# An encoder layer on one core: the first phase in six pieces instead of five, half of the turned input copied by ScalarE, late constants sent for after the first weights

## The reference

```python
cond = jax.nn.silu(c)
mod = cond @ w_ada[l] + b_ada[l]
sh1, sc1, gt1, sh2, sc2, gt2 = jnp.split(mod, N_MOD, axis=-1)
hn = modulated_rms_norm(h, sh1, sc1)     # rms_norm(x) * (1 + sc1) + sh1
proj = hn @ w_in[l]
```

## Time and profile before

| | us |
|---|---|
| median of 3 runs | 2613.78 |
| lowest, highest | 2613.31, 2613.84 |
| profiled execution | 2611.63 |
| its span | 2610.0 |
| PE busy in the span | 2517.7 (96%) |
| DVE busy | 1477.6 (57%) |
| ACT busy | 903.4 (35%) |

### The profile page before, as it was taken

One profiled execution on the slowest core, in us unless ns is written; L12 is line 12 of the kernel. 1 busy time (PEld: TensorE's weight loads), 2 busy tenths in 40 slices (PEclk: granted clock), 3 DMA queues, 4 the chain that ended last, 5 costly groups with the idle time before them and its releaser, 6 DMA issues.

```text
span 2610.0 us, 34653 instructions
## 1 busy us (share of the span) xinstructions
PE 2517.7 (96%) x11920; PEld 2060.3 (79%) x11920; DVE 1477.6 (57%) x1917; ACT 903.4 (35%) x1274; POOL 201.7 (8%) x278
## 2 busy tenths in 40 slices
PE   4999999999999899989999999999999999999997
PEld 4777787787787678868888888888888888888786
DVE  6837678678678584474444444444444444444454
ACT  4334424424424334342222222222222222222344
POOL 3401121111121021000000000000000000000000
PEclk7999999999999899999999999999999999999998
DMA  9933454454454355323333333323333333333233
GB/s 353 324 109 113 131 161 128 133 158 130 135 157 129 109 145 153 97 73 98 96 96 88 104 97 96 96 88 98 104 96 97 96 89 96 100 96 96 87 95 130
DMA packets 431728, 318.20 MB, mean 122 GB/s; under 512 B 12950, under 2 KB 403905, under 8 KB 431169
## 3 DMA queue, kind: packets, MB, share of 16 engines
q1 hardware_dynamic: 401712, 212.19, 28.2%
q0 software_dynamic: 29184, 104.87, 12.4%
q10 hardware_dynamic: 785, 0.51, 0.1%
HBM read 313.33 MB, written 4.19 MB: 122 GB/s over the span
## 4 chain that ended last, share of the span: by engine, by line
PE 89%; DVE 6%; issue 2%; ACT 1%; DMA 1%; POOL 0%; DVEq 0%; ACTq 0%; POOLq 0%
PE pw L1474 23%; PE pw L1476 22%; PE pw L1475 22%; PE pw L1458 2%; PE pw L1460 2%; PE pw L1459 2%; PE pd L1791 2%; PE pd L1768 1%; PE pd L1783 1%; DMA ka<-in_w_ada_dram 1%; DVE w_lo L969 1%; PE pd L1731 1%; PE pd L1808 1%; PE pd L1803 1%; DVE ada_acc L985 1%
## 5 line engine op out<-in xcount | busy, mean ns | idle before, releaser
L1474 PE MATMUL pw<-act_hi,w_hi 128*128 128x512 f32 x1984 | 793.8, 400 | 3.8 <-DVE w_lo L969 3.0
L969 DVE TENSOR_TENSOR w_lo<-raw,w_hi 128x1024 fp32r<-128x1024 f32 x426 | 524.0, 1230 | 481.4 <-ACT w_hi L573 475.0
L1476 PE MATMUL pw<-act_hi,w_lo 128*128 128x512 f32 x1984 | 774.3, 390 | 0.0
L1475 PE MATMUL pw<-act_lo,w_hi 128*128 128x512 f32 x1984 | 773.1, 390 | 0.0
L573 ACT ACTIVATE w_hi<-raw 128x1024 fp32r<-128x1024 f32 x426 | 450.2, 1057 | 542.9 <-PE pw L1476 444.6
L1474 PEld LDWEIGHTS pw<-act_hi,w_hi 128*128 128x128 f32 x1984 | 373.2, 188 | 90.2 <-issue 16.4
L1475 PEld LDWEIGHTS pw<-act_lo,w_hi 128*128 128x128 f32 x1984 | 373.2, 188 | 81.4 <-issue 6.9
L1476 PEld LDWEIGHTS pw<-act_hi,w_lo 128*128 128x128 f32 x1984 | 372.8, 188 | 78.8
L1474 PE MATMUL pw<-mh_hi,w_hi 128*128 128x512 f32 x704 | 276.1, 392 | 3.0 <-DVE w_lo L969 3.0
L1476 PE MATMUL pw<-mh_hi,w_lo 128*128 128x512 f32 x704 | 274.2, 389 | 0.0
L1475 PE MATMUL pw<-mh_lo,w_hi 128*128 128x512 f32 x704 | 274.0, 389 | 0.0
(11 more groups left out here) (291 smaller groups left out, 2469.8 us busy)
## 6 DMA issues: line engine op xcount, KB each, us to landing
raw<-in_w_up_dram SPq DMA_DIRECT2D x172, 512.0 KB, 4.0
ada_w<-in_w_ada_dram POOLq DMA_DIRECT2D x128, 512.0 KB, 4.6
raw<-in_w_in_dram SPq DMA_DIRECT2D x84, 512.0 KB, 3.9
raw<-in_w_down_dram SPq DMA_DIRECT2D x64, 384.0 KB, 3.4
raw<-in_w_down_dram SPq DMA_DIRECT2D x64, 320.0 KB, 3.2
raw<-in_w_out_dram SPq DMA_DIRECT2D x32, 512.0 KB, 4.6
DD<-in_w_ada_dram POOLq DMA_DIRECT2D x9, 512.0 KB, 8.0
EG<-in_w_ada_dram POOLq DMA_DIRECT2D x9, 512.0 KB, 6.7
```

The source lines that it names most:

```text
L969: V.tensor_tensor(w_lo[slot][:], raw[slot][:], w_hi[slot][:].bitcast(F32), ALU.subtract).then_inc(lo_made.sem, 1)
L1474: M(bank, w_hi[slot][:, k, :], hi[:, k0 + k, :], start=first, stop=False)
L1475: M(bank, w_hi[slot][:, k, :], lo[:, k0 + k, :], start=False, stop=False)
L1476: ins = M(bank, w_lo[slot][:, k, :], hi[:, k0 + k, :], start=False, stop=last)
```

## The change

The first piece of four feature tiles becomes two pieces of two, so there are six. The copies of x blocks 2 and 3 move from VectorE to ScalarE, with signals of their own. The late constants are issued after the gate weights. `normed` for tiles 0 and 1 stands behind step i = 10 of the second piece, the low halves of the first two weight units behind its steps 8 and 9. The products on tiles 0 and 1 are made for units 0 and 1 only, the rest of these units when tiles 2 and 3 are there; unit 2 takes all four tiles at once. Four signals of x become one that counts steps.

```diff
-PIECES = ((0, 4), (4, 8), (8, 12), (12, 14), (14, 16))
+PIECES = ((0, 2), (2, 4), (4, 8), (8, 12), (12, 14), (14, 16))
...
-            sp.dma_start(cst[:, C_FIRST:C_N], A["shape_constants"][:, C_FIRST:C_N]).then_inc(more_in, 16)
...
             sp.dma_start(wba, w_in[:, COL_BA:COL_BA + 32].rearrange("(k p) n -> p k n", p=P)).then_inc(ba_in, 16)
+            sp.dma_start(cst[:, C_FIRST:C_N], A["shape_constants"][:, C_FIRST:C_N]).then_inc(more_in, 16)
...
+            def x_block(b):
+
+                for q in range(4):
+                    act.wait_ge(*xt_sum.after(0, 4 * b + q + 1))
+                    nc.scalar.activation(x_feat[:, 4 * q:4 * q + 4, b * P:(b + 1) * P], blocks(pd[q]), ACT.Copy).then_inc(x_copied.sem, 1)
+
+            x_block(2)
             split(0, 0, ahead=False)
+            x_block(3)
             split(0, 1, ahead=False)
...
-            act.wait_ge(ba_in, 16)
-            nc.scalar.activation(wba_hi[:], wba, ACT.Copy).then_inc(ba_split.sem, 1)
             act.wait_ge(*x_turned.after(0))
+            act.wait_ge(*x_copied.after(0))
...
             first_halves(0)
+            act.wait_ge(ba_in, 16)
+            nc.scalar.activation(wba_hi[:], wba, ACT.Copy).then_inc(ba_split.sem, 1)
+            first_halves(1)
             first_split(2)
             first_split(3)
-            first_halves(1)
+            first_halves(2)
...
-                if i in (2, 4, 6, 8):
-                    x_block((2, 4, 6, 8).index(i))
-                if i in (10, 11):
-                    low(0, i - 10)
-
-            def ahead(j, lows):
+                if i in (5, 8):
+                    x_block((5, 8).index(i))
+
+            def ahead(j, lows, at_row=2):
...
-                    if 2 <= i < 2 + len(tiles):
-                        normed(tiles[i - 2])
-                    if i == 6 and j == 1:
+                    if at_row <= i < at_row + len(tiles):
+                        normed(tiles[i - at_row])
+                    if i == 13 and j == 1:
...
-            ahead(1, {7: 2, 11: 3})
-            ahead(2, {5: 4, 8: 5, 12: 6})
-            ahead(3, {5: 7, 9: 8, 13: 9})
-            ahead(4, {5: 10})
+            ahead(1, {8: 0, 9: 1}, at_row=10)
+            ahead(2, {7: 2, 11: 3})
+            ahead(3, {5: 4, 8: 5, 12: 6})
+            ahead(4, {5: 7, 9: 8, 13: 9})
+            ahead(5, {5: 10})
...
                 for q in range(4):
-                    if b:
+                    if b == NB - 1:
+                        pe.wait_ge(*x_copied.after(0, q + 1))
+                    elif b:
                         pe.wait_ge(*x_turned.after(0, 4 * (b - 1) + q + 1))
...
-            for j in range(3):
+            first_unit(0, 0, 2, end=False)
+            first_turned(1, TURNED_ROWS[0])
+            first_unit(1, 0, 2, end=False)
+            first_turned(1, TURNED_ROWS[1])
+            first_sums(1)
+            first_unit(0, 2, 4)
+            first_turned(2, TURNED_ROWS[0])
+            first_unit(1, 2, 4)
+            first_turned(2, TURNED_ROWS[1])
+            ba_part(0, 4)
+            first_unit(2, 0, 4)
+            first_sums(2)
+            for j in (2, 3):
                 k0, k1 = PIECES[j]
-                first_unit(3 * j, k0, k1)
+                first_unit(3 * j - 3, k0, k1)
                 first_turned(j + 1, TURNED_ROWS[0])
-                first_unit(3 * j + 1, k0, k1)
-                if j:
+                first_unit(3 * j - 2, k0, k1)
+                if j == 3:
                     ba_part(*PIECES[j - 1])
                 first_turned(j + 1, TURNED_ROWS[1])
-                first_unit(3 * j + 2, k0, k0 + 2, end=False)
+                first_unit(3 * j - 1, k0, k0 + 2, end=False)
                 first_sums(j + 1)
-                first_unit(3 * j + 2, k0 + 2, k1)
+                first_unit(3 * j - 1, k0 + 2, k1)
```

More of the change, by code:

```diff
@@ L378, in build @@
         cols_sum, cols_made, cond_made = signal("cols_sum"), signal("cols_made", 2), signal("cond_made")
-        more_in, c_sum, x_turned = sem("more_in"), signal("c_sum"), signal("x_turned", KT)
+        more_in, c_sum, x_turned = sem("more_in"), signal("c_sum"), signal("x_turned", 2 * NB)
         ba_split, ba_row_sum, ba_row_taken = signal("ba_split", 2), signal("ba_row_sum"), signal("ba_row_taken")
         gate_row_sum, gates_made = signal("gate_row_sum"), signal("gates_made", 2)
-        x_squared, x_rstd = signal("x_squared", NB), signal("x_rstd", 2 * NB)
-        x_normed, xt_sum = signal("x_normed", NB), signal("xt_sum", KT)
+        x_step, x_copied, xt_sum = signal("x_step", 4 * NB), signal("x_copied", 2 * NB), signal("xt_sum", KT)
         hn_full, hn_hi, hn_lo = signal("hn_full", KT), signal("hn_hi", KT), signal("hn_lo", KT)
@@ L592, in _ @@
                 if b:
-                    act.wait_ge(*x_squared.after(0, b))
-                nc.scalar.activation(junk, x_in[:, b, :], ACT.Square, accum_out=nrm[:, 0, b:b + 1]).then_inc(x_squared.sem, 1)
-                act.wait_ge(*x_squared.after(0, b + 1))
+                    act.wait_ge(*x_step.after(0, 4 * b - 3))
+                nc.scalar.activation(junk, x_in[:, b, :], ACT.Square, accum_out=nrm[:, 0, b:b + 1]).then_inc(x_step.sem, 1)
+                act.wait_ge(*x_step.after(0, 4 * b + 1))
                 if b == 0:
                     act.wait_ge(consts_in, 16)
[L598 to L601, removed]
+                nc.scalar.activation(nrm[:, 1, b:b + 1], nrm[:, 0, b:b + 1], ACT.Ln, scale=1.0 / DM, bias=eps1).then_inc(x_step.sem, 1)
+                act.wait_ge(*x_step.after(0, 4 * b + 2))
+                nc.scalar.activation(nrm[:, 2, b:b + 1], nrm[:, 1, b:b + 1], ACT.Exp, scale=-0.5).then_inc(x_step.sem, 1)
+                act.wait_ge(*x_step.after(0, 4 * b + 3))
                 nc.scalar.activation(x_in[:, b, :], x_in[:, b, :], ACT.Identity, scale=nrm[:, 2, b:b + 1]) \
-                    .then_inc(x_normed.sem, 1)
+                    .then_inc(x_step.sem, 1)
+            def x_block(b):
[3 more added lines that the diff above has]
+            x_block(2)
             split(0, 0, ahead=False)
+            x_block(3)
             split(0, 1, ahead=False)
@@ L636, in _ @@
             first_split(6)
-            first_halves(2)
+            first_halves(3)
             first_split(7)
@@ L640, in _ @@
             first_split(9)
-            first_halves(3)
+            first_halves(4)
             first_split(10)
             first_split(11)
-            first_halves(4)
+            first_halves(5)
             first_split(12)
@@ L978, in first_add @@
                     if j == 1:
-                        dve.wait_ge(*x_squared.after(0))
+                        dve.wait_ge(*x_step.after(0, 4 * NB - 3))
                     elif j >= 2:
@@ L1534, in x_turn @@
             def x_turn(b):
-                pe.wait_ge(*x_normed.after(0, b + 1))
+                pe.wait_ge(*x_step.after(0, 4 * b + 4))
                 for q in range(4):
-                    if b:
+                    if b == NB - 1:
+                        pe.wait_ge(*x_copied.after(0, q + 1))
+                    elif b:
                         pe.wait_ge(*x_turned.after(0, 4 * (b - 1) + q + 1))
@@ L1560, in _ @@
             pe.wait_ge(*x_turned.after(0))
+            pe.wait_ge(*x_copied.after(0))
             def first_unit(u, k0, k1, end=True):
@@ L1586, in ba_part @@
                     ins.then_inc(ba_row_sum.sem, 1)
[L1588 removed]
+            first_unit(0, 0, 2, end=False)
[11 more added lines that the diff above has]
+            for j in (2, 3):
                 k0, k1 = PIECES[j]
[L1590 removed]
+                first_unit(3 * j - 3, k0, k1)
                 first_turned(j + 1, TURNED_ROWS[0])
[L1592 to L1593 removed]
+                first_unit(3 * j - 2, k0, k1)
+                if j == 3:
                     ba_part(*PIECES[j - 1])
                 first_turned(j + 1, TURNED_ROWS[1])
[L1596 removed]
+                first_unit(3 * j - 1, k0, k0 + 2, end=False)
                 first_sums(j + 1)
[L1598 removed]
+                first_unit(3 * j - 1, k0 + 2, k1)
             first_unit(9, 12, 14)
[L1600 removed]
+            first_turned(5, TURNED_ROWS[0])
             first_unit(10, 12, 14, end=False)
[L1602 to L1604 removed]
+            first_turned(5, TURNED_ROWS[1])
+            first_sums(5)
+            ba_part(*PIECES[3])
             first_unit(10, 14, 16)
@@ L1640, in _ @@
             pe.wait_ge(more_in, 16)
-            pe.wait_ge(*first_out.after(4))
+            pe.wait_ge(*first_out.after(5))
             pe.wait_ge(*gate_v.after(0, 4))
```

## The result

| | before | changed |
|---|---|---|
| median, us (12 runs each) | 2613.77 | 2620.91 |
| lowest, highest | 2612.04, 2614.55 | 2617.66, 2622.49 |
| span of the profiled execution | 2610.0 | 2620.7 |
| start of the sums of tiles 8 to 11 | 102.90 | 112.31 |
| start of the last sums | 143.23 | 154.90 |

The changed kernel is slower, by a ratio of 1.0028 (95% interval 1.002 to 1.0036), 7.1 us. I had forecast +2.4 us and a range that ended at 2620.0. Its profiled execution was the slowest of its twelve (2622.5), and that of the kernel before (2611.63) was faster than all of its twelve, so the traces show some 9 to 12 us of delay where the medians differ by 7. The changed kernel also scatters more than the one before: 4.8 us from lowest to highest against 2.5.

The account below looks back on a forecast made before the run. DMA, PE and DVE all at their limit at 60 to 100 us; the end follows the sums of tiles 8 to 11. Their start +0.8 us without a clock fall, +2.8 with one; taken +2.4: 2616.2 us, range 2610.0 to 2620.0.

Parts of the forecast that it names:

- first columns: Columns of the first narrow piece out at 37.6 us, against 53.5 before.
- first product: PE's first product at 48.6 us, behind `normed` and 1 us for late constants; 7.4 us before the earlier 55.98.
- sums of tiles 2, 3 end: After 24 products (7.3 us) and three groups of eight columns (2.5 us) on PE: 58.4 us.
- From then DVE is what counts.: From the seventh row, near 21.3 us, DVE's steps and copies set the pace: 35 us, columns out at 37.6.
- a rival with 0.09: Full 7.4 us head start reaches the end; transfers fill DVE's wait at 53 us, DMA sets the pace: 2606.4; chance 0.09.
- PE's early products: 24 products ahead of the sums of tiles 2 and 3, nine at 0.43 and fifteen at 0.23: 7.3 us.
- The standstill at the second columns: DVE, two steps into the next piece, stands at `first_columns` from 53.3 to 58.7 us: 5.4 us idle, 0.99 before.
- From the second to the third sums: PE restarts at 61.1 us and ends the sums of tiles 4 to 7 at 80.5, or 82.5 with a clock fall.
- Rival B: PE's clock falls in every new gap, sums of tile 8 at half pace: +5.3 to +8, 2619 to 2622; chance 0.13.
- Whatever the start moves by, the end moves by: From the sums of tiles 8 to 11 on, work order is unchanged, so the end shifts as much as their start.
- Packets in turn.: At 10 to 20 us DMA engines alternate queues by packet; halved w_ada packets make a narrow row land every 3.1 us.
- Rival D: Columns no earlier as w_ada starves behind x, rows over 4 us: columns at 42, +4 to +5, 2618; chance 0.08.

Follow-up runs that it names:

- x2: Changed kernel with PE's sums of tiles 2 and 3 ahead of unit 1's products, those of tiles 4 to 7 mid unit 2; 2615.09 us.
- x12: x9 plus ten half buffers, two narrow rows per buffer, for the last two narrow pieces; 2605.49 us.
- x11: Kernel before the change, with four buffers for rows of w_ada instead of five; 2621.38 us.
- x7: x2 plus ten half buffers, two narrow rows per buffer, for the two narrow pieces at the start; 2612.98 us.
- x10: Changed kernel, but PE makes no product before tiles 0 to 3 are all summed; six pieces stay; 2615.27 us.
- x3: Changed kernel plus twelve unread 128x384 products in each of the PE gaps before tiles 2 and 4; 2623.3 us.
- x1: Changed kernel with the late constants issued behind x and ahead of the first weight units, as before the change; 2621.69 us.
- x14: Changed kernel with ten half buffers for its last two narrow pieces alone; 2615.64 us.
- x13_six_halves: x2 (six pieces, sums ahead) plus ten half buffers for all four narrow pieces, first and last; 2608.49 us.
- x9: Kernel before (five pieces) plus ScalarE copying blocks 2 and 3 and late constants behind the gate weights; no split; 2610.65 us.

## Why the prediction was wrong

The sign was right (+2.4 forecast), the size was a third of the +7.1 measured, and the range ended 0.9 us short. By its steps, against the trace of the changed kernel (the errors are taken against the forecast without a fall of the clock):

| step | forecast | trace | error added |
|---|---|---|---|
| first columns | 37.6 | 40.0 | +2.4 |
| first product | 48.6 | 50.5 | -0.5 |
| sums of tiles 2, 3 end | 58.4 | 61.5 | +1.2 |
| sums of tiles 4 to 7 end | 80.5 (82.5 with one fall of the clock) | 88.7 | +5.1 |
| sums of tiles 8 to 11 start | 103.7 (105.7) | 112.3 | +0.4 |

- **"From then DVE is what counts."** This is one of the two steps that failed. It took DVE's steps as back to back from the seventh row on, and DMA as hidden behind them. The first five rows came in four steps of 2.35 us (8.98 to 18.39) while x streamed, faster than the 3.1 forecast. But then DVE waited 4.13 us for the seventh row, used at 23.27 us and not near 21.3, and 2.83 us for the row at 38.09 us, which stands ahead of the first columns; PE had its sums done at 36.4 us, as forecast. (The sum has a slip too: nine narrow steps were put at 6.7 us and took 7.2.) For the constants I had 0 to 2.7 us and took 1. The share of 1.04 in the earlier trace rows was in my hand, for a rival with 0.09: DMA sets the pace as well, though not everywhere, for from 38.09 to 53.69 us DVE ran on without a wait. That rival drew the wrong end from it, that DMA would fill DVE's wait. It can't: a row can only be sent for when DVE has used the one five before. DVE's standstill, small transfers, a buffer less: each stops the stream, and with it what comes after. x2, x12 and x11 show the three one by one in time; x7 shows the second at the start in bytes only.
- **PE's early products were sized nearly right and worth nothing.** The 24 products took 8.1 us and not 7.3, since twelve and not nine ran at the half clock; that is most of the 1.2 in the third row. Without them the time is the same (x10).
- **The standstill at the second columns was named, but its size came out by luck** (5.4 us forecast, all of it for PE). DVE stood 2.78 us for PE, half of that, because before it 3.0 us had gone in waits for two rows that I had taken as landed. Putting the sums first brings 5.8 us (x2; 5.5 us, each against the kernel before beside it), twice the wait that the trace has there. The bytes per us after 52 us say that the standstill also stops the transfers; how much of the 5.8 us is that and how much is PE's gaps and clock is not separated. Two more lines, PE's order or VectorE's, would have kept it out.
- **From the second to the third sums I was 5.1 us short.** This is the other step that failed, and the larger term. Here PE's queue came last: DVE had its last step done at 83.1 us, PE started the sums at 86.82, 22.6 us after 64.23, where I had 17.7 (61.1 to 80.5, less the sums themselves). The clock read 0.50 from 64 to 70 us and 0.60 from 76 to 80 us: 6 + 3.2 us at the lower level, 4.6 us of work lost, of which by this reading the 3.7 us between 83.1 and 86.8 lie on the path. I had taken one fall at 2 us. It is a reading of the trace and not shown: x3, where the first of the two falls was shorter, got only 0.2 us of it back. DVE's twelve steps took 21.3 us instead of 19.8, with 1.95 us of waits for rows.
- **Rival B**, the clock in every gap, had 0.13 and 2619 to 2622 us, which holds the measured time, and part of its sign is in the trace: 52 to 100 us ran at a mean clock of 0.78 against 0.92 (0.88 in the trace of x1). The other part is not: the sums of tile 8 took 1.95 us, not the 3.6 of half pace. And it is not the whole: the bytes are missing before 52 us already, and x11 has the same loss with rows that come late at the full clock. How much of the 7 us is the clock's is **open**: x3, made to tell, had 0.86 in that stretch and no gain, yet a fall of its own on the path. x2 had 0.92; its order both frees DVE from the products at half pace and keeps PE going, and these two are not separated.
- **"Whatever the start moves by, the end moves by"** held roughly: +9.4 at the sums of tile 8, +11.7 at the last sums, +10.7 in the span. The last two narrow pieces add some: DVE waits 2.76 and 1.21 us for rows there. x14 shows both losses add up.
- **Packets in turn.** The engines do take the queues in turn by packet, as the Trainium skill has it in "DMA: Bandwidth & Descriptors", section Queues, rings and completion order. The changed kernel shows it again, 10 to 20 us (packets, MB, share):

```profile
q1 hardware_dynamic: 354, 2.55, 65.5%
q0 software_dynamic: 354, 1.18, 30.4%
```

But the size that I put into the rule was wrong. A narrow row didn't come in packets of half the size: 1.18 MB in 354 packets are 3.3 KB each, against 3.7 KB in the earlier trace rows. It came in about half as many. So w_ada lost 9% of its bytes there, not nearly half, and a row came every 2.35 us, near the 2 us that I had kept for shares by bytes. What does speak against the change is something that the turns alone don't give: with the engines full, 20 to 36 us ran at a share of 1.05 and 336 GB/s instead of 384. The same page of the Trainium skill advises in its section Rules for kernel authors to coalesce many small transfers into one large. The stretches of x13_six_halves and x12_both_halves, with rows of 256 and 512 KB, point the same way: 342 against 376 GB/s, both full (the last section takes them apart).

- **Rival D** (rows starved behind x, columns at 42 us) is out in its form: the first rows came early. The delay came after x was in.

The split's 10.3 us (x9 to the changed kernel), as far as taken apart: 5.8 the order of PE's queue, 2.1 the bytes in flight at the start, and 2.3 more to x9. Each against the kernel before beside it, these are 5.5, 1.3 and 2.7 of 9.5 us. The first is clear of noise, the second is not. The third stands at 3.0 in the other pair (x13 to x12); whether it is the fewer bytes per us of full engines or VectorE's narrow steps is open.

## What to carry to other kernels

When a stretch shows DMA, VectorE and PE all near full, moving one engine's work earlier may bring nothing, as here; count bytes per us before and after, and ask of each wait whether it keeps a buffer from being sent for again. Halving a transfer with the same number of buffers halves what is in flight: split the buffers too. In PE's queue, put the short sums that others wait for ahead of the long products that nobody waits for.

## What the hardware showed that I had not expected

- Full DMA engines (share 1.04 to 1.06) carried fewer bytes with rows of 256 KB than with rows of 512 KB. All packets and those of `w_ada` (q0) in x13_six_halves, then in x12_both_halves, 20 to 36 us:

```profile
DMA packets 3849, 5.46 MB, mean 342 GB/s; under 512 B 1694, under 2 KB 2868, under 8 KB 3844
q0 software_dynamic: 1224, 4.00, 72.6%
...
DMA packets 2753, 6.01 MB, mean 376 GB/s; under 512 B 417, under 2 KB 1610, under 8 KB 2742
q0 software_dynamic: 1275, 4.64, 77.4%
```

Two things are in this. The small pieces of the gate weights fall into this stretch in x13 (1694 packets under 512 B against 417) and mostly into the next one in x12. But the rows themselves are slower too: 4.00 MB in 72.6% of 16 us are 344 GB/s of the time spent on them, 4.64 MB in 77.4% are 375; from 36 to 52 us it is 346 against 379.

- One buffer of 512 KB fewer out of five (plus two) cost 8.3 us in 110 us of streaming, though VectorE, which uses them, was busy for 92% of the time from 60 to 100 us.
- The clock fell while PE had work. PE's timeline of x2_sums_first, the last row there before which it stood still:

```profile
70.86 1.95 PE L1537 MATMUL pd<-cond,va 128*128 128x1 f32 x16 [2.02 <-DMA va<-in_w_ada_dram]
```

From there on it is busy, with these 128x1 columns and then with products, yet from 72 to 78 us the clock goes down and comes back (all engines, same columns as above):

```profile
72.00:74.00 2.00, 2.00 (x14) 1.38 (x14) 1.71 (x2) 0.00 (x0) 0.95 (x2) 0.95 0.99 367
74.00:76.00 2.00, 2.00 (x7) 0.71 (x6) 2.00 (x3) 0.00 (x0) 1.21 (x2) 0.50 1.08 381
76.00:78.00 2.00, 2.00 (x8) 1.42 (x7) 1.19 (x1) 0.00 (x0) 0.51 (x1) 0.70 1.03 386
```

In x3_warm the fall at 62 to 64 us had only 0.32 us of idle time and a row of 128x1 columns ahead of it. So my count of new idle gaps was no count of falls.
